# Query norm as the scale of the exponential, norm gains folded into k, one wide product for k's squares, in a two-layer trunk on one Trainium2 core

## The chip, the core and the metric

The kernel runs on one of the eight cores of a Trainium2 chip. A core has a matrix engine (TensorE, PE in the rows; its weight loads are the rows PEld), a vector engine (VectorE, DVE), a scalar engine (ScalarE, ACT), GpSimd (POOL) and SyncE (SP), which here only issues transfers. Each engine runs its own instructions in the order in which they were written, and they wait for each other at counting semaphores. Matrix products land in eight PSUM banks of 128 x 512 float32. The metric is the device time of one launch in microseconds (us), the median over runs.

## The reference, cut to what matters

Two residual layers over 512 tokens of width 1024. Layer 0 mixes tokens by a convolution module, layer 1 by differential attention; each is followed by a mixture of 32 gated-MLP experts (two experts for each token), whose weights, 6 MB for each expert and layer, are read from device memory. Everything is float32. The change is in the attention alone:

```
q = rms_norm(q.reshape(B, S, N_HEADS, 2, HEAD_DIM), q_g) * (HEAD_DIM ** -0.5)
k = rms_norm(k.reshape(B, S, N_HEADS, 2, HEAD_DIM), k_g)
s = einsum("bhcqd,bhckd->bhcqk", qb, kb)
p = softmax(where(mask, s, -inf), axis=-1)          # block-causal mask
a = p[:, :, 0] - lam * p[:, :, 1]
o = rms_norm(einsum("bhqk,bhkd->bhqd", a, vb), subln_g) * (1 - lambda_init)
```

There are 8 heads; each has two components (c = 0, 1) of 64 channels for q and k, and 128 channels of v. `rms_norm` divides each vector of 64 channels by the root of its mean square (plus 1e-6) and multiplies by a gain for each channel. For a fixed query the reciprocal root of q is one number for each row of scores.

## The kernel before

The span falls into these parts: layer 0's convolution (to about 300 us), its experts (to about 820), attention (840 to 1130), the output product with residual and routing (to 1210), layer 1's experts (to the end). In both expert parts the weights stream through a ring of six 2 MB units and four spare buffers. The stream is issued by SyncE: each unit's transfer waits for the semaphore of the work that last used its buffer. For layer 1's experts the first four units wait for `v_ready` and `qk_ready` of the attention (slots that held q, k, v weights); the next two and the first spare wait for the last `mix_ready`, the end of the output product; the rest follow the routing and the experts.

The attention is a software pipeline over 10 stages (`attention_steps()`): stage st projects q, k, v of head h = st, does scores, softmax and the weighted sum of head g = st - 1, and normalises the output of head e = st - 2. Stages 1 to 7 have both an h and a g; the scores of head 7 fall in stage 8, which has no projection and in its place runs part of the output product (`output_ahead`, L1474). The order on each engine is written out by hand; nothing is scheduled automatically.

On TensorE, a stage is: `scores(i)` for four query blocks i, i+1, i+2, i+3 of 128 rows (the widths are 128, 256, 384, 512 keys), with the four halves of the q and k projections (`qk_half`, L1380) between them; `transposed` (L1443) turns the combined probabilities `a`, which VectorE made, and `weighted` (L1454) multiplies them with v. `transposed(i + 3)` stands right behind `weighted(i + 2)`, then come `sum_squares` of k, half of v's projection (`v_half`, L1413), `spread_rs` (L1401), `weighted(i + 3)`, `output_T` (L1462), and the other half of v. Then the next stage begins with the scores of the head just projected, which wait for its normalised q and k (`qk_done`).

The norm of q and k goes like this. ScalarE squares the projected tile out of PSUM (channels are partitions, 512 tokens are columns) and copies it, times the gain, to SBUF (`qk_g_sb`, L734). TensorE sums the squares over channels with the squares as the stationary operand and two columns of `halves` as the moving one, four small products for each of q and k (L1391): the result has tokens as partitions, 128 x 16. ScalarE takes roots (L794), VectorE reciprocals (L1122). VectorE then widens the result to 128 x 512 (L1124), and TensorE turns it back to channels as partitions with eight products against the identity (`spread_rs`), so that VectorE can multiply (L1104).

The softmax of one query block goes: `maxima` (DVE, L1083: the negated row maximum of both components) gives `m_done`; ACT takes two exponentials with the maximum as bias and the row sum accumulated (L749); `combine` (DVE, L1089 to L1094) makes `a` from the two; PE transposes it.

Of the kernel before, what the change touches and what calls it, by code (L numbers as in the profile page):

```python
# [65 lines left out]
def trunk(nc, x, norm1_g, norm2_g, conv_w_in, conv_b_in, conv_dw, conv_dw_b, conv_ln_g, conv_ln_b,  # L66
# [11 lines left out]
    with ctx:  # L78
# [44 lines left out]
        def small_at(a, n=1):  # L123
# [26 lines left out]

        qk_ready, qk_sq, qk_ss, qk_root, qk_rec, qk_rs_ready, qk_scaled, qk_done = (
            sem("qk_ready"), sem("qk_sq"), sem("qk_ss"), sem("qk_root"), sem("qk_rec"), sem("qk_rs_ready"),
            sem("qk_scaled"), sem("qk_done"))
        v_ready, v_done = sem("v_ready"), sem("v_done")
# [111 lines left out]
        qk_sqb = [area1[:, c * T:(c + 1) * T] for c in range(2)]  # L266
        qk_rs_wide = [area1[:, (4 + c) * T:(5 + c) * T] for c in range(2)]
        qk_g_sb = [area1[:, (2 + c) * T:(3 + c) * T] for c in range(2)]
        p_sb = [scratch[:, b * 1024:(b + 1) * 1024].rearrange("p (c k) -> p c k", c=2) for b in range(3)]
# [5 lines left out]
        qk_bank = [bank[2], bank[3]]  # L275
        ss_bank = bank[4][:, 0:4 * NT]
        rs_bank = [bank[4], bank[1]]
        v_bank, aT_bank, o_bank = bank[5], bank[6], bank[7]
# [3 lines left out]
        o_ssq = scratch[:, 5280:5280 + 32]  # L282
        o_std = scratch[:, 5312:5312 + 32]
        o_r = scratch[:, 5344:5344 + 32]
        o_rn = scratch[:, 5376:5376 + 32]
        o_junk = scratch[:, 5408:5408 + P]
        qk_std = scratch[:, 5536:5536 + 4 * NT]
        qk_rs = scratch[:, 5552:5552 + 4 * NT]

# [311 lines left out]
        def _(act):  # L601
# [165 lines left out]
            for h, g, e in attention_steps():  # L767
                if g is not None:
                    i = NT * g
                    take_v(g)  # L770
                    probabilities(i)
                    take_aT(i)
                    probabilities(i + 1)
                if h is not None:
                    qk_square(h, 0)
                if g is not None:
                    take_aT(i + 1)
                    probabilities(i + 2)
                if e is not None:
                    o_squares(e)  # L780
                if g is not None:
                    take_aT(i + 2)
                    probabilities(i + 3)
                if h is not None:
                    qk_square(h, 1)
                if g is not None:
                    take_aT(i + 3)
                if e is not None:
                    act.wait_ge(o_sq, NT * (e + 1))
                    cols = slice(NT * e, NT * (e + 1))  # L790
                    a.activation(o_std[:, cols], o_ssq[:, cols], ACT.Sqrt, bias=eps[:], scale=1.0 / P).then_inc(on_std, 1)
                if h is not None:
                    act.wait_ge(qk_ss, 2 * (h + 1))
                    a.activation(qk_std, ss_bank, ACT.Sqrt, bias=eps[:], scale=1.0 / HEAD_DIM).then_inc(qk_root, 1)  # L794

# [6 lines left out]
        def _(dve):  # L802
# [263 lines left out]

            link(v.tensor_scalar(qk_g[:, 0:1], qk_g[:, 0:1], HEAD_DIM ** -0.5, None, ALU.mult))
            link(v.tensor_scalar(sub_g[:], sub_g[:], 1.0 - LAMBDA_INIT, None, ALU.mult))
# [11 lines left out]
            def maxima(i):  # L1080
                W = P * (pairs[i][1] + 1)
# [19 lines left out]

            def norm_qk(h, c):
                dve.wait_ge(qk_rs_ready, 2 * h + c + 1)
                v.tensor_tensor((qT, kT)[c][h % 2], qk_g_sb[c], rs_bank[c][:], ALU.mult).then_inc(qk_done, 1)  # L1104

            for h, g, e in attention_steps():
                if g is not None:
                    i = NT * g
                    maxima(i)
                    combine(i)  # L1110
                    maxima(i + 1)
                    combine(i + 1)
                    take_o(i)
                    maxima(i + 2)
                    combine(i + 2)
                    take_o(i + 1)
                    maxima(i + 3)
                    combine(i + 3)
                    take_o(i + 2)
                if h is not None:  # L1120
                    dve.wait_ge(qk_root, h + 1)
                    link(v.reciprocal(qk_rs, qk_std))  # L1122
                    for c in range(2):
                        v.tensor_copy(qk_rs_wide[c].rearrange("p (k f) -> p k f", f=HEAD_DIM),  # L1124
                                      qk_rs[:, 2 * NT * c:2 * NT * (c + 1)].unsqueeze(2).to_broadcast([P, 2 * NT, HEAD_DIM])
                                      ).then_inc(qk_rec, 1)
                if e is not None:
                    dve.wait_ge(on_std, e + 1)
                    cols = slice(NT * e, NT * (e + 1))
                    link(v.reciprocal(o_rn[:, cols], o_std[:, cols]))  # L1130
                    v.tensor_tensor(oh[e % 2], oh[e % 2], o_rn[:, cols].unsqueeze(2).to_broadcast([P, NT, P]),
                                    ALU.mult).then_inc(on_done, 1)
                if h is not None:
                    norm_qk(h, 0)
                if g is not None:
                    take_o(i + 3)
                if h is not None:
                    norm_qk(h, 1)
# [9 lines left out]
        def _(pe):  # L1148
# [223 lines left out]
            def qk_half(h, c, half):  # L1372

                u = n0 + 3 * (h // 4) + c
                if half == 0:
                    loaded(pe, u)
                    if h >= 1:
                        pe.wait_ge(qk_scaled, 2 * h - 1 + c)
                for k in range(4 * half, 4 * half + 4):
# [3 lines left out]

            def sum_squares(h, c):

                pe.wait_ge(qk_sq, 2 * h + c + 1)
                if c == 0 and h >= 1:
                    pe.wait_ge(qk_done, 2 * h - 1)
                for t in range(NT):
                    k = 2 * (NT * c + t)  # L1390
                    last = mm(ss_bank[:, k:k + 2], qk_sqb[c][:, t * P:(t + 1) * P], halves[:, 0:HEAD_DIM + 1:HEAD_DIM],  # L1391
                              start=True, stop=True)
                last.then_inc(qk_ss, 1)

            def spread_rs(h, c):

                pe.wait_ge(qk_rec, 2 * h + c + 1)
                if c == 1 and h >= 1:
                    pe.wait_ge(p_done, 2 * NT * h)
# [78 lines left out]
            for h, g, e in attention_steps():  # L1478
# [19 lines left out]
                if h is not None:  # L1498
                    qk_half(h, 1, 0)
                    sum_squares(h, 0)  # L1500
                if last_head:
# [15 lines left out]
                if h is not None:  # L1517
                    sum_squares(h, 1)
                    v_half(h, 0)
                if h is not None:  # L1520
                    spread_rs(h, 0)
                    spread_rs(h, 1)
                if last_head:
# [35 lines left out]
```

## Time and profile before

| | |
|---|---|
| median of 3 runs | 1717.74 us (1713.15 to 1719.24) |
| the profiled execution, device time | 1716.26 us |
| its span | 1714.5 us |
| mean granted TensorE clock | 0.919 of 2.4 GHz |
| PE matmul busy | 1420.8 us, 83% |
| DVE busy | 441.6 us, 26% |
| ACT busy | 328.2 us, 19% |
| the chain that ended last | PE 49%, DMA 33%, DVE 7%, POOL 4% |

The busy shares are averages over parts with different limits. The chain is read from the last instruction back to what released each step; its largest entries are the transfers of expert weights (31%) and the experts' first products (L1272, 19%), followed by the q and k projections of the attention (L1380, 7%). Ends of matmuls are modelled, so PE rows of a few hundredths of a microsecond are not exact.

### The profile page before, as it was taken

How to read it: one execution, taken by the hardware profiler on the slowest of the kernel's cores; microseconds unless marked ns; L12 is line 12 of the kernel's file. 1: busy time of each engine (PE TensorE's matmuls, PEld its weight loads, DVE VectorE, ACT ScalarE, POOL GpSimd, SP SyncE). 2: the span in 40 equal slices, each digit the busy share in tenths (PEclk: the TensorE clock that was granted, in tenths of full speed). 3: DMA queues.
4: the chain of work that ended last, by engine and by line, in shares of the span. 5: the costliest groups of instructions: out<-in, count | busy, mean ns of one | idle time of the engine just before them, and what ended most of it. 6: DMA issues, size and time to landing. Idle time of an engine off the chain costs nothing.

```text
span 1714.5 us, 17059 instructions
## 1 busy us (share of the span) xinstructions
PE 1420.8 (83%) x6028; PEld 645.3 (38%) x6028; DVE 441.6 (26%) x858; ACT 328.2 (19%) x629; POOL 278.0 (16%) x381
## 2 busy tenths in 40 slices
PE   4996696998888788887599999986997888888883
PEld 2442243332333233232376676644332322232331
DVE  1799614111110110110333333423211101101112
ACT  2555311010000000000334434421000000000000
POOL 0688100121111111110000000000121111111100
PEclk9998796999999899998799999987999999999997
DMA  9122005789999999998600400305799999999995
GB/s 337 21 98 98 1 37 239 294 363 418 421 420 420 420 420 419 418 416 335 247 1 1 148 1 2 147 25 230 309 365 420 420 419 421 419 418 416 414 414 205
DMA packets 91249, 473.13 MB, mean 276 GB/s; under 512 B 19675, under 2 KB 19675, under 8 KB 40260
## 3 DMA queue, kind: packets, MB, share of 16 engines
q1 hardware_dynamic: 78500, 443.12, 63.7%
q0 software_dynamic: 10400, 16.82, 2.6%
q10 hardware_dynamic: 2304, 12.58, 1.9%
q8 instruction: 29, 0.48, 0.1%
q14 instruction: 16, 0.13, 0.0%
HBM read 466.43 MB, written 23.33 MB: 286 GB/s over the span
## 4 chain that ended last, share of the span: by engine, by line
PE 49%; DMA 33%; DVE 7%; POOL 4%; issue 3%; SPq 3%; ACT 1%; ACTq 0%; POOLq 0%; DVEq 0%
DMA ring<-in_moe_w 31%; PE banks L1272 19%; PE banks L1380 7%; PE banks L1221 5%; POOL scratch L515 4%; PE banks L1289 3%; PE banks L1413 3%; SPq L315 2%; DVE banks L863 2%; PE banks L1170 2%; PE banks L1474 1%; PE banks L1427 1%; PE banks L1454 1%; DMA area<-y_dram 1%; PE banks L1239 1%
## 5 line engine op out<-in xcount | busy, mean ns | idle before, releaser
L1272 PE MATMUL banks<-ring,scratch 128*64 128x512 f32 x1984 | 503.6, 659 | 142.4 <-DMA ring<-in_moe_w 131.6
L1272 PEld LDWEIGHTS banks<-ring,scratch 128*64 128x64 f32 x1984 | 158.7, 150 | 483.5 <-issue 483.3
L1289 PE MATMUL banks<-ring,scratch 128*64 128x512 f32 x1008 | 231.7, 602 | 3.0 <-DVE scratch L1006 3.0
L1006 DVE COPY scratch<-banks 128x256 f32<-128x256 f32 x65 | 27.6, 425 | 799.7 <-PE banks L1280 799.7
L680 ACT ACTIVATE scratch<-banks 64x512 f32<-64x512 f32 x65 | 38.3, 589 | 597.6 <-PE banks L1272 597.6
L533 POOL COPY at_out<-rows_out 128x1 int32 (+1 forms) x64 | 11.7, 183 | 703.6 <-ACT scratch L684 703.6
L515 POOL TENSOR_TENSOR scratch<-scratch 128x512 f32<-128x512 f32 x88 | 112.0, 1273 | 62.0 <-ACT scratch L652 50.0
L1380 PE MATMUL banks<-hT,ring 128*128 128x512 f32 x256 | 117.9, 604 | 0.8 <-DVE hT L820 0.8
L1170 PE MATMUL banks<-hT,ring 128*128 128x512 f32 x256 | 112.5, 600 | 0.7 <-issue 0.7
L1289 PEld LDWEIGHTS banks<-ring,scratch 128*64 128x64 f32 x1008 | 68.4, 137 | 118.6 <-issue 111.6
L1221 PE MATMUL banks<-ring,area 128*128 128x512 f32 x200 | 99.0, 650 | 10.6 <-ACT area L662 9.6
L684 ACT ACTIVATE scratch<-banks 128x512 f32<-128x512 f32 x65 | 38.8, 597 | 285.8 <-PE banks L1289 285.8
L863 DVE SCALAR_TENSOR_TENSOR banks<-scratch,chan,banks 128x512 f32<-128x512 f32 x128 | 85.0, 750 | 0.0
L525 POOL DMA_INDIRECT scratch<-xn_dram,at_in x64 | 67.2, 1051 | 56.2 <-POOL at_in L522 53.9
L652 ACT ACTIVATE scratch<-scratch,chan 128x512 f32<-128x512 f32 x96 | 66.7, 718 | 49.1 <-POOL scratch L515 35.3
L543 POOL MEMSET scratch<- 128x512 f32 x4 | 2.1, 525 | 455.4 <-DVE x_res L892 455.3
L536 POOL DMA_INDIRECT y_dram<-scratch,at_out x64 | 65.8, 1028 | 56.5 <-POOL at_out L533 56.5
L1170 PEld LDWEIGHTS banks<-hT,ring 128*128 128x128 f32 x256 | 49.2, 193 | 62.7 <-issue 62.7
L1380 PEld LDWEIGHTS banks<-hT,ring 128*128 128x128 f32 x256 | 46.2, 189 | 49.5 <-issue 46.9
L1221 PEld LDWEIGHTS banks<-ring,area 128*128 128x128 f32 x200 | 40.1, 208 | 60.9 <-issue 56.0
L1413 PE MATMUL banks<-ring,hT 128*128 128x128 f32 x512 | 60.4, 276 | 0.0
L1158 PE MATMUL banks<-ident,area 128*128 128x128 f32 x128 | 26.1, 367 | 39.3 <-ACT area L624 34.3
(205 smaller groups left out, 1185.0 us busy)
## 6 DMA issues: line engine op xcount, KB each, us to landing
ring<-in_moe_w SPq DMA_DIRECT2D x374, 1024.0 KB, 17.1
area<-in_moe_w SPq DMA_DIRECT2D x12, 1024.0 KB, 14.7
ring<-in_attn_w_qkv SPq DMA_DIRECT2D x12, 1024.0 KB, 14.5
ring<-in_conv_w_in SPq DMA_DIRECT2D x8, 1024.0 KB, 14.6
area<-y_dram ACTq DMA_DIRECT2D x8, 1024.0 KB, 7.9
ring<-in_conv_w_out SPq DMA_DIRECT2D x4, 1024.0 KB, 12.4
xn_dram<-area ACTq DMA_DIRECT2D x8, 512.0 KB, 2.6
hT<-in_moe_w SPq DMA_DIRECT2D x4, 1024.0 KB, 12.4
```

The costliest lines, as they stand in the source:

```text
L515: g.tensor_tensor(pacc[ct % 2], pacc[ct % 2], tap[(k - 1) % TAP_BUFS], ALU.add).then_inc(tap_added, 1)
L525: g.indirect_dma_start(out=xe[s], out_offset=None, in_=xn_dram[l][:, :], in_offset=bass.IndirectOffsetOnAxis(ap=at_in[:, s:s + 1], axis=0) ...
L536: g.indirect_dma_start(out=y_dram[l][:, :], out_offset=bass.IndirectOffsetOnAxis(ap=at_out[:, s:s + 1], axis=0), in_=y_sb[s], in_offset=No ...
L652: a.activation(dst, u_buf[ct % 2][:, w:w + T], ACT.Copy, scale=chan[:, ct, w:w + 1]).then_inc(tap_made, 1)
L684: a.activation(y_sb[s], bank[6 + s][:], ACT.Copy).then_inc(sems["y_taken"], 1)
L863: ins = v.scalar_tensor_tensor(dst, ub[:, w:w + T], chan[:, ct, w:w + 1], acc, ALU.mult, ALU.add)
L1170: last = mm(dst, w[:, c, cols], src[:, c, :], start=start and c == 0, stop=stop and c == NC - 1)
L1221: last = mm(dst[:], src[:, c, t * P:(t + 1) * P], w_chunks(n0 + n)[:, c, :], start=c == 0, stop=c == NC - 1 and not bias)
L1272: last = mm(bank[2 + s][q * SLOTS:(q + 1) * SLOTS, :], xeT[s][:, j, h, :], w[:, c, :], start=c == 0, stop=c == NC - 1)
L1289: last = mm(bank[6 + s][q * SLOTS:(q + 1) * SLOTS, :], hidT[s][:, j, :], w2c[:, j, q * 512:(q + 1) * 512], start=j == 0, stop=j == 3)
L1380: last = mm(qk_bank[c][:], w_chunks(u)[:, k, (h % 4) * P:(h % 4 + 1) * P], hT[:, k, :], start=k == 0, stop=k == NC - 1)
L1413: last = mm(v_bank[:, t * P:(t + 1) * P], hT[:, k, t * P:(t + 1) * P], w_chunks(u)[:, k, (h % 4) * P:(h % 4 + 1) * P], start=k == 0, stop= ...
```

## The change

The two components of q are no longer normalised before the scores. Their reciprocal roots stay as a 128 x 8 tile with tokens as partitions (`q_rs`), where each column is the per-partition scale of one exponential; the negated maximum, which is the bias, has to be multiplied by the same number first. Both gains and the factor 1/8 go into one gain vector for k. The squares of k are summed by one product, with `halves` stationary and the 512 columns of squares moving, into the score bank 0; that result already stands in channels as partitions, spread over all 64 of each component, so nothing has to be widened or turned. ScalarE then takes 128 x 512 roots, VectorE 128 x 512 reciprocals, and one more VectorE instruction multiplies k out of PSUM by gain and reciprocal. `spread_rs` and `sum_squares` of k are gone.

```
 def qk_square(h, c):                                   # ACT
     act.wait_ge(qk_ready, 2 * h + c + 1)
     a.activation(qk_sqb[c], qk_bank[c][:], ACT.Square).then_inc(qk_sq, 1)
-    if h >= 1:
-        act.wait_ge(qk_done, 2 * h - 1 + c)
-    a.activation(qk_g_sb[c], qk_bank[c][:], ACT.Copy, scale=qk_g[:, c:c + 1]).then_inc(qk_scaled, 1)
+    if c == 0:
+        a.activation(qT[h % 2], qk_bank[0][:], ACT.Copy).then_inc(q_copied, 1)
...
 def probabilities(i):                                  # ACT
-        a.activation(p_sb[i % 3][:, c, 0:W], score[:, c, 0:W], ACT.Exp, bias=mx[:, i, c:c + 1],
+        a.activation(p_sb[i % 3][:, c, 0:W], score[:, c, 0:W], ACT.Exp, bias=mx_scaled[:, i % 4, c:c + 1],
+                     scale=q_rs[h % 2][:, 2 * b + c:2 * b + c + 1],
                      accum_out=ps[:, i, c:c + 1]).then_inc(p_done, 1)
...
-                    act.wait_ge(qk_ss, 2 * (h + 1))
-                    a.activation(qk_std, ss_bank, ACT.Sqrt, ...).then_inc(qk_root, 1)
+                    act.wait_ge(q_ss, h + 1)
+                    a.activation(q_std, q_ss_bank, ACT.Sqrt, ...).then_inc(q_root, 1)
+                    act.wait_ge(k_ss, h + 1)
+                    a.activation(k_std, k_ss_bank[:], ACT.Sqrt, ...).then_inc(k_root, 1)
...
 def maxima(i):                                         # DVE
-    v.tensor_reduce(mx[:, i, :], score[:, :, 0:W], AX.X, ALU.max, negate=True).then_inc(m_done, 1)
+    link(v.tensor_reduce(mx[:, i, :], score[:, :, 0:W], AX.X, ALU.max, negate=True))
+    v.tensor_tensor(mx_scaled[:, i % 4, :], mx[:, i, :], q_rs[h % 2][:, 2 * b:2 * b + 2], ALU.mult).then_inc(m_done, 1)
...
-def norm_qk(h, c):                                     # DVE
-    dve.wait_ge(qk_rs_ready, 2 * h + c + 1)
-    v.tensor_tensor((qT, kT)[c][h % 2], qk_g_sb[c], rs_bank[c][:], ALU.mult).then_inc(qk_done, 1)
+def scale_q(h):
+    dve.wait_ge(q_root, h + 1)
+    v.reciprocal(q_rs[h % 2], q_std).then_inc(q_rs_done, 1)
+
+def norm_k(h):
+    dve.wait_ge(k_root, h + 1)
+    link(v.reciprocal(k_rs, k_std))
+    v.scalar_tensor_tensor(kT[h % 2], qk_bank[1][:], qk_g[:, 1:2], k_rs, ALU.mult, ALU.mult).then_inc(k_done, 1)
...
-def spread_rs(h, c):                                   # PE
-    for t in range(NT):
-        last = mm(rs_bank[c][:, t * P:(t + 1) * P], qk_rs_wide[c][:, t * P:(t + 1) * P], ident[:], start=True, stop=True)
-    last.then_inc(qk_rs_ready, 1)
+def k_squares(h):
+    pe.wait_ge(qk_sq, 2 * h + 2)
+    pe.wait_ge(q_copied, h + 1)
+    mm(k_ss_bank[:], halves[:], qk_sqb[1], start=True, stop=True).then_inc(k_ss, 1)
...
 def scores(i):                                         # PE
     if b == 0:
-        pe.wait_ge(qk_done, 2 * (h + 1))
+        pe.wait_ge(q_copied, h + 1)
+        pe.wait_ge(k_done, h + 1)
...
                 if g is not None:
                     transposed(i + 3)
                 if h is not None:
-                    sum_squares(h, 1)
+                    k_squares(h)
                     v_half(h, 0)
-                if h is not None:
-                    spread_rs(h, 0)
-                    spread_rs(h, 1)
```

`link` makes VectorE wait for its own instruction. `q_squares(h)` is the old `sum_squares(h, 0)`.

The order on TensorE, in the second half of a stage. The kernel before (L1380 projections, L1454 weighted sums, L1443 transposes, L1391 sums of squares, L1413 v, L1401 `spread_rs`, L1462 output transposes, L1427 and L1431 the next stage's first scores with their mask):

```order
L1380 MATMUL banks_3<-hT,ring 128x512 x4
L1454 MATMUL banks_7<-area,scratch 128x128 x3
L1443 MATMUL banks_7<-ident,scratch 128x128 x4
L1391 MATMUL banks_5<-halves,area 128x2 x4
L1413 MATMUL banks_5<-ring,hT 128x128 x16
L1401 MATMUL banks_5<-ident,area 128x128 x4
L1401 MATMUL banks_1<-ident,area 128x128 x4
L1454 MATMUL banks_7<-area,scratch 128x128 x4
L1462 MATMUL banks_7<-ident,area 128x128 x4
L1413 MATMUL banks_5<-ring,hT 128x128 x16
L1427 MATMUL banks_1<-area 128x128 x2
L1431 MATMUL banks_1<-mask_col,mask_row 128x64 x2
```

And the same place in the changed kernel, whose line numbers have moved a little (L1383 projections, L1401 now the one wide product, L1412 v):

```order
L1383 MATMUL banks_3<-hT,ring 128x512 x4
L1454 MATMUL banks_7<-area,scratch 128x128 x3
L1443 MATMUL banks_7<-ident,scratch 128x128 x4
L1401 MATMUL banks_1<-area,halves 128x512
L1412 MATMUL banks_5<-ring,hT 128x128 x16
L1454 MATMUL banks_7<-area,scratch 128x128 x4
L1462 MATMUL banks_7<-ident,area 128x128 x4
L1412 MATMUL banks_5<-ring,hT 128x128 x16
L1427 MATMUL banks_1<-area 128x128 x2
L1431 MATMUL banks_1<-mask_col,mask_row 128x64 x2
```

Eight products against the identity and four small sums are gone, and one product of 128 x 512 stands in their place, ahead of v's first half.

The order on VectorE, from the last combination of a stage to the first combination of the next. Before (L1094 the combination, L1100 scaling of the output, L1122 and L1124 the reciprocals and their widening, L1130 and L1131 the output norm, L1104 the multiplication of q and of k, L1141 the output's gain, L1083 the row maximum):

```order
L1094 SCALAR_TENSOR_TENSOR scratch<-scratch 128x512
L1100 TENSOR_SCALAR area<-banks_7,scratch 128x128
L1122 RECIPROCAL scratch<-scratch 128x16
L1124 COPY area<-scratch 128x512 x2
L1130 RECIPROCAL scratch<-scratch 128x4
L1131 TENSOR_TENSOR area<-area,scratch 128x512
L1104 TENSOR_TENSOR area<-area,banks_5 128x512
L1100 TENSOR_SCALAR area<-banks_7,scratch 128x128
L1104 TENSOR_TENSOR area<-area,banks_1 128x512
L1141 TENSOR_SCALAR area<-banks_7,sub_g 128x512
L1083 TENSOR_REDUCE scratch<-banks_1 128x2
L1089 RECIPROCAL scratch<-scratch 128x1
```

The changed kernel at the same place (L1109 the reciprocal for q, L1113 and L1114 the norm of k, L1087 and L1088 the row maximum and its multiplication):

```order
L1099 SCALAR_TENSOR_TENSOR scratch<-scratch 128x512
L1105 TENSOR_SCALAR area<-banks_7,scratch 128x128
L1109 RECIPROCAL scratch<-scratch 128x8
L1135 RECIPROCAL scratch<-scratch 128x4
L1136 TENSOR_TENSOR area<-area,scratch 128x512
L1113 RECIPROCAL area<-area 128x512
L1114 SCALAR_TENSOR_TENSOR area<-banks_3,qk_g,area 128x512
L1105 TENSOR_SCALAR area<-banks_7,scratch 128x128
L1144 TENSOR_SCALAR area<-banks_7,sub_g 128x512
L1087 TENSOR_REDUCE scratch<-banks_1 128x2
L1088 TENSOR_TENSOR scratch<-scratch 128x2
L1094 RECIPROCAL scratch<-scratch 128x1
```

The widening copies and the two multiplications have given way to a reciprocal of the full 128 x 512 and one multiplication, both ahead of the last scaling of the output; and a small multiplication has come behind each row maximum.

## Rows read from the trace of the kernel before

**Rows 1.** Stretches: us; each engine's busy us (instructions); granted clock, DMA share, GB/s.
```profile
963.90:996.50 32.60, 32.60 (x188) 22.23 (x188) 12.64 (x32) 13.56 (x37) 0.00 (x0) 1.00 0.18 67
1094.50:1129.50 35.00, 32.91 (x119) 16.39 (x119) 12.10 (x30) 13.01 (x41) 0.00 (x0) 1.00 0.17 61
```

**Rows 2.** Waits of SyncE's queue: total us, times, longest us.
```profile
SPq L315 <- PE banks L1380: 232.3, 3, 115.6
```

**Rows 3.** The chain, whole span: start us, us, what.
```profile
1275.90 18.52 DMA ring<-in_moe_w
```

**Rows 4.** The chain inside stage 4, 963.9 to 996.5 us.
```profile
980.50 3.63 PE banks L1380 x8
984.80 0.51 PE banks L1443 x4
985.31 0.79 PE banks L1391 x8
...
989.78 1.79 PE banks L1401 x16
...
996.47 0.30 PE banks L1427
```

**Rows 5.** Timeline of ScalarE, stage 4: start us, us, what, [idle before, releaser].
```profile
964.45 1.28 ACT L749 ACT_TABLE_LOAD   x1
...
981.80 0.69 ACT L749 ACTIVATE scratch<-banks,scratch 128x512 f32<-128x512 f32 x1 [1.99 <-DVE scratch L1083]
...
985.35 0.60 ACT L765 ACTIVATE scratch<-banks 128x512 f32<-128x512 f32 x1
...
987.46 0.26 ACT L794 ACTIVATE scratch<-banks,eps 128x16 f32<-128x16 f32 x1
```

**Rows 6.** Timeline of ScalarE at the convolution's layer norm, 180 to 200 us.
```profile
186.90 0.72 ACT L659 ACTIVATE area<-area,eps 128x512 f32<-128x512 f32 x1 [3.42 <-DVE area L878]
...
192.49 0.81 ACT L662 ACTIVATE area<-area,chan 128x512 f32<-128x512 f32 x1 [3.57 <-DVE area L883]
```

**Rows 7.** Timeline of VectorE, stage 4.
```profile
964.42 0.42 DVE L1083 TENSOR_REDUCE scratch<-banks 128x2 f32<-128x256 f32 x1 [2.98 <-PE banks L1431]
...
966.85 0.27 DVE L1091 TENSOR_SCALAR scratch<-scratch,small 128x1 f32<-128x1 f32 x1
...
971.30 0.48 DVE L1094 SCALAR_TENSOR_TENSOR scratch<-scratch 128x256 f32<-128x256 f32 x1
...
980.54 1.22 DVE L1083 TENSOR_REDUCE scratch<-banks 128x2 f32<-128x1024 f32 x1 [1.19 <-PE banks L1431]
...
983.85 0.75 DVE L1094 SCALAR_TENSOR_TENSOR scratch<-scratch 128x512 f32<-128x512 f32 x1
...
988.92 0.69 DVE L1131 TENSOR_TENSOR area<-area,scratch 128x512 f32<-128x512 f32 x1
```

**Rows 8.** Timeline of VectorE just ahead of the attention.
```profile
841.89 0.16 DVE L1077 TENSOR_TENSOR small<-small 128x1 f32<-128x1 f32 x1 [0.27 <-ACT small L727]
```

**Rows 9.** Timeline of PE weight loads, stage 4.
```profile
967.56 0.14 PEld L1443 LDWEIGHTS banks<-ident,scratch 128*128 128x128 f32 x1 [0.38 <-DVE scratch L1094]
...
984.65 0.42 PEld L1443 LDWEIGHTS banks<-ident,scratch 128*128 128x128 f32 x4
```

**Rows 10.** Timeline of PE matmuls: stage 0, and the second transpose of stage 4.
```profile
855.98 1.05 PE L1391 MATMUL banks<-halves,area 128*128 128x2 f32 x8 [0.69 <-ACT area L731]
...
972.60 0.38 PE L1443 MATMUL banks<-ident,scratch 128*128 128x128 f32 x2
```

**Rows 11.** Timeline of VectorE at the convolution's layer norm, 187 to 192 us.
```profile
187.65 3.35 DVE L880 RECIPROCAL area<-area 128x512 f32<-128x512 f32 x1 [0.79 <-ACT area L659]
191.04 0.69 DVE L882 TENSOR_TENSOR area<-area 128x512 f32<-128x512 f32 x1
```

**Rows 12.** The page's costliest groups: count | busy us, mean ns | idle before.
```profile
L863 DVE SCALAR_TENSOR_TENSOR banks<-scratch,chan,banks 128x512 f32<-128x512 f32 x128 | 85.0, 750 | 0.0
```

**Rows 13.** ScalarE in stage 8: the wait ahead of the last probabilities' copy.
```profile
1118.84 0.60 ACT L765 ACTIVATE scratch<-banks 128x512 f32<-128x512 f32 x1 [5.46 <-PE banks L1443]
```

More of the change, by code:

```diff
@@ L149, in trunk @@
             sem("picks_done"), sem("ranks_ready"), sem("hot_done"), sem("lists_ready"), sem("lists_done"))
-        qk_ready, qk_sq, qk_ss, qk_root, qk_rec, qk_rs_ready, qk_scaled, qk_done = (
-            sem("qk_ready"), sem("qk_sq"), sem("qk_ss"), sem("qk_root"), sem("qk_rec"), sem("qk_rs_ready"),
-            sem("qk_scaled"), sem("qk_done"))
+        qk_ready, qk_sq, q_ss, k_ss, q_copied, q_root, k_root, q_rs_done, k_done = (
+            sem("qk_ready"), sem("qk_sq"), sem("q_ss"), sem("k_ss"), sem("q_copied"), sem("q_root"), sem("k_root"),
+            sem("q_rs_done"), sem("k_done"))
         v_ready, v_done = sem("v_ready"), sem("v_done")
@@ L266, in trunk @@
         qk_sqb = [area1[:, c * T:(c + 1) * T] for c in range(2)]
-        qk_rs_wide = [area1[:, (4 + c) * T:(5 + c) * T] for c in range(2)]
-        qk_g_sb = [area1[:, (2 + c) * T:(3 + c) * T] for c in range(2)]
+        k_rs = area1[:, 4 * T:5 * T]
+        k_std = area1[:, 2 * T:3 * T]
         p_sb = [scratch[:, b * 1024:(b + 1) * 1024].rearrange("p (c k) -> p c k", c=2) for b in range(3)]
@@ L275, in trunk @@
         qk_bank = [bank[2], bank[3]]
-        ss_bank = bank[4][:, 0:4 * NT]
-        rs_bank = [bank[4], bank[1]]
+        q_ss_bank = bank[4][:, 0:2 * NT]
+        k_ss_bank = bank[0]
         v_bank, aT_bank, o_bank = bank[5], bank[6], bank[7]
@@ L283, in trunk @@
         o_std = scratch[:, 5312:5312 + 32]
+        mx_scaled = scratch[:, 5560:5560 + 8].rearrange("p (i c) -> p i c", c=2)
+        q_std = scratch[:, 5552:5552 + 2 * NT]
         o_r = scratch[:, 5344:5344 + 32]
@@ L286, in trunk @@
         o_junk = scratch[:, 5408:5408 + P]
-        qk_std = scratch[:, 5536:5536 + 4 * NT]
-        qk_rs = scratch[:, 5552:5552 + 4 * NT]
+        q_rs = [scratch[:, 5536 + 2 * NT * b:5536 + 2 * NT * (b + 1)] for b in range(2)]
         ahead = (0, 4)
@@ L792, in _ @@
                 if h is not None:
-                    act.wait_ge(qk_ss, 2 * (h + 1))
-                    a.activation(qk_std, ss_bank, ACT.Sqrt, bias=eps[:], scale=1.0 / HEAD_DIM).then_inc(qk_root, 1)
+                    act.wait_ge(q_ss, h + 1)
+                    a.activation(q_std, q_ss_bank, ACT.Sqrt, bias=eps[:], scale=1.0 / HEAD_DIM).then_inc(q_root, 1)
+                    act.wait_ge(k_ss, h + 1)
+                    a.activation(k_std, k_ss_bank[:], ACT.Sqrt, bias=eps[:], scale=1.0 / HEAD_DIM).then_inc(k_root, 1)
             route(1)
@@ L1120, in _ @@
                 if h is not None:
[L1121 to L1126, printed above, removed]
+                    scale_q(h)
                 if e is not None:
@@ L1377, in qk_half @@
                     if h >= 1:
-                        pe.wait_ge(qk_scaled, 2 * h - 1 + c)
+                        pe.wait_ge((q_copied, k_done)[c], h)
                 for k in range(4 * half, 4 * half + 4):
@@ L1382, in qk_half, with q_squares @@
                     last.then_inc(qk_ready, 1)
[L1384 to L1388, printed above, removed]
+            def q_squares(h):
+                pe.wait_ge(qk_sq, 2 * h + 1)
+                if h >= 1:
+                    pe.wait_ge(q_root, h)
                 for t in range(NT):
-                    k = 2 * (NT * c + t)
-                    last = mm(ss_bank[:, k:k + 2], qk_sqb[c][:, t * P:(t + 1) * P], halves[:, 0:HEAD_DIM + 1:HEAD_DIM],
+                    last = mm(q_ss_bank[:, 2 * t:2 * t + 2], qk_sqb[0][:, t * P:(t + 1) * P], halves[:, 0:HEAD_DIM + 1:HEAD_DIM],
                               start=True, stop=True)
-                last.then_inc(qk_ss, 1)
-            def spread_rs(h, c):
-                pe.wait_ge(qk_rec, 2 * h + c + 1)
-                if c == 1 and h >= 1:
-                    pe.wait_ge(p_done, 2 * NT * h)
-                for t in range(NT):
-                    last = mm(rs_bank[c][:, t * P:(t + 1) * P], qk_rs_wide[c][:, t * P:(t + 1) * P], ident[:], start=True, stop=True)
-                last.then_inc(qk_rs_ready, 1)
+                last.then_inc(q_ss, 1)
+            def k_squares(h):
+                pe.wait_ge(qk_sq, 2 * h + 2)
+                pe.wait_ge(q_copied, h + 1)
+                mm(k_ss_bank[:], halves[:], qk_sqb[1], start=True, stop=True).then_inc(k_ss, 1)
             def v_half(h, half):
@@ L1499, in _ @@
                     qk_half(h, 1, 0)
-                    sum_squares(h, 0)
+                    q_squares(h)
                 if last_head:
```

9 lines of the change are left out of this document (4 added, 5 removed).

## The prediction, made before the changed kernel was run

> **What bounds the kernel now.** I read the whole span first: in the chain that ended last, transfers of expert weights hold the largest share and the matrix engine the next. So the first question is which of the two sets the time where the change is. The busy times by stretch answer it: stage 4 of the attention lasts 32.6 us and PE's matmuls are busy for 32.60 of them at clock 1.00, while DVE is busy for 12.64 and ACT for 13.56 [rows 1]. The attention's seven stages with both a projection and a softmax are a PE queue without gaps; an instruction taken out of it shortens the span by its own length, if nothing comes late instead.
>
> The second question is whether the time comes back further on. SyncE's queue waits 232.3 us in total, three times, for the q and k projections [rows 2]: the weight stream stands still in the attention, because its next buffers are held. All but four of layer 1's units start from the end of the output product or later, and the first wait of PE for a weight transfer in layer 1's experts is at 1275.90 [rows 3]. From there the stream sets the pace; it starts with the output product, so it moves with the attention's end. The four units that start inside the attention land before they are wanted, so they hide nothing.
>
> The third view is the chain inside a stage, for the price of each group as it stands on the path, and the fourth the timelines of ACT and DVE, to see what becomes late.
>
> **The change on PE.** `spread_rs` goes: 1.79 us a stage on the chain [rows 4]. `sum_squares` of k, 0.79 us [rows 4], goes too, but the wide product comes in its place. It has the shape of a projection product, 128 x 512 in float32, and four of these take 3.63 us [rows 4]: 0.91 us for one. So the wide product is no gain, it costs 0.12 us more than the four narrow ones. Bounds: 0.79 (no dearer than what it replaces), and 1.17 if its end isn't covered by the next product, as the group of L1391 shows 1.05 us as a duration beside 0.79 on the chain [rows 4, 10]. I take 0.91, the nearest shape. Net for each head: 1.79 - 0.12 = 1.67 us. Stage 0 has the same two edits, and its wait of 0.69 us for the squares [rows 10] stays. Eight heads: 13.4 us.
>
> **The change on the softmax chain.** Between row maximum and exponential stands a new multiplication of 128 x 2, linked to the one before. The nearest row, a small linked tensor-tensor, is 0.16 us [rows 8]; with the step of about 0.03 between linked instructions, 0.19 us. The dearest small one in the chain is 0.27 [rows 7], which gives the upper end 0.31; it can't be below 0.19 by much, since it is serial work.
>
> Each exponential gets a second per-partition operand, the scale beside the bias. The trace has no exponential with both. It has a 128 x 512 Sqrt with a bias operand in 0.72 us and a Silu with bias and scale operands in 0.81 [rows 6]: 0.09 more. The lower end is nothing, if the difference lies in the function. I take 0.09, twice per block, so 0.18. A block's combination is thus 0.37 us later (0.19 to 0.49).
>
> Who waits for it: the transposes. For the fourth block, the combination ends at 983.85 + 0.75 = 984.60 [rows 7] and the weight load of its transposes starts at 984.65 [rows 9]. There is 0.05 of slack, and everything on PE is queued behind it: the sum for k, v, the weighted sum, the next scores. So PE waits 0.32 us there, in stages 1 to 7: 2.2 us (1.0 to 3.1). For the second block the combination ends at 971.78 [rows 7] and its transposes start at 972.60 [rows 10]: 0.82 of slack covers 0.37, and the third has more. For the first block the loader waits for DVE already [rows 9]; but there the maximum is ready at 964.84 [rows 7] while ACT's table load runs until 965.73 [rows 5], so the multiplication is hidden, and only the 0.18 of the exponentials is left. The load, 0.14 long, then ends by 967.88, about when the products ahead of it end (the second block's scores follow without a gap), so I count nothing; exposed it would cost 7 x 0.18 = 1.3. In stage 8 ACT waits 5.46 us for the last block's transposes, which stand behind `output_ahead` [rows 13]: there the delay costs nothing.
>
> **The change on the k path.** In place of the small chain there is ACT root, DVE reciprocal, DVE multiplication, all 128 x 512, and the next scores wait for it. By stage 4, with PE 0.32 later from 984.65 on: the wide product starts at 985.63 and ends at 986.54. ACT copies the transposed block (0.60), loads the root's table (1.28), and reaches q's roots at 987.46 + 0.32 = 987.78 [rows 5]. That takes 0.26 [rows 5], then k's roots 0.60 to 0.72 [rows 5, 6], done by 988.7. DVE does the small reciprocals and the output norm, 0.69 [rows 7], until about 989.25. The reciprocal of 128 x 512 is the price to look up: 3.35 us [rows 11], until 992.6; the multiplication out of PSUM 0.75 [rows 12], until 993.4. PE reaches the next scores at 996.47 [rows 4] - 1.67 + 0.32 = 995.1. The margin is 1.7 us, so nothing is charged, and it holds in stage 0 too, where the squares are ready at 855.98 [rows 10] and v's two halves alone (3.6 us each) follow: k done at about 862.3, PE there at 864.1. DVE's last scaling of the output and the output's gain move behind the norm of k, to about 994.5; their readers on PE come after the next stage's first scores and projection quarter, at 999, and DVE's next maximum is wanted at 995.7. ACT loses one gain copy a stage. These I count at nothing, covered by the same 1.7 us.
>
> **Sum.** -13.4 + 2.2 = -11.2 us on the profiled execution's 1716.26: 1705.1. What lies outside its span, 1.8 us, stays. The median of the runs shown is 1.5 us above that execution, so a median should be between 1705.1 and 1706.6; I say 1706. With all ends: gain 8 x (1.79 + 0.79 - 1.17) - 3.1 = 8.2 at the least, 8 x 1.79 - 1.0 = 13.3 at the most, 1703 to 1708 from the profiled execution.
>
> **Rivals.** (A) The softmax chain becomes the bound in more places: the first block's 0.18 is exposed (1.3 us), the multiplication and the wide product are at their upper ends. Gain 8.2 - 1.3 = 6.9, time 1709 to 1711. For it: the loader already waits at the first block [rows 9] and the fourth has 0.05 us. Against: the values I took come from near shapes. (B) The gain at its upper end or past it: the exponential's second operand is free and the wide product is no dearer than the four: 1703. (C) The weight stream hides the gain: it would have to be running through the attention's end. Rows 2 and 3 speak against it; the time would be 1716 to 1718, and also if the change did not shorten PE's queue as its order shows.
>
> (D) Slower: a long Vector instruction holds its linked successor for about its own length again. The multiplication behind a 1.22 us maximum [rows 7] would start 1.22 later, which is 7 x 1.22 = 8.5 us on PE, and k's multiplication 3.35 later, which passes the margin of 1.7 by 1.65 in 8 stages, 13.2 us. Sum -11.2 + 8.5 + 13.2 = +10.5: 1727. It decides as soon as the gap behind the reciprocal passes 1.7 us; with both it is slower than before when they add over 11.2 us. Against it: the reciprocal that starts at 187.65 and lasts 3.35 ends at 191.00, and its linked successor starts at 191.04 [rows 11]. The Trainium skill, page "VectorE: DVE Perf Modes", section "The DRAIN you can't avoid", speaks for this rival, if its drain is taken to lie behind the duration in the rows: it says that each Vector instruction is followed by a drain of about its duration less 266 ns, and that the next can't start until the pipe is empty. By its figure the gaps would be 0.96 and 3.09 us, and the sum, as an estimate from that page, 1723. The rows just named disagree with that reading, 0.04 us against 3.09, so the chance is small.
>
> **How the numbers follow.** Forecast 0.60, A 0.21, B 0.10, C 0.05, D 0.04. About 0.5%, 8.6 us, is what a measurement can tell from no change; that bound lies at 1709.1. The forecast and B lie beyond it but for the spread of the runs, which is 3 us either way; A lies on it. Faster by over 0.5%: 0.72; within: 0.23; slower: 0.05. The likeliest case alone is 1702 to 1710. The range adds A and the spread: 1700 to 1713.
>
> **What would show it.** Right: stages 1 to 7 of 31.3 us, L1401 as one product with two records of 0.45 on the chain, the reciprocal L1113 at 3.35, the next scores without a wait for L1114, PE's loader waiting for L1099 at the fourth block by about 0.3. Exponentials of 512 in 0.77. Wrong: PE idle ahead of the scores with releaser L1114 (k's path), a stage of 31.8 or more with waits for L1099 (rival A), or the attention 11 us shorter while the end of the span does not move (C).

## The result and the profile after

The changed kernel takes 1708.41 us (median of 9 runs, 1704.09 to 1711.11), the kernel before 1717.74 (9 runs, 1712.93 to 1721.85). The ratio is 0.9939, 95% interval 0.9925 to 0.9954: 10.5 us less (7.9 to 12.9); the two medians by themselves lie 9.3 us apart. Two more measurements of the same pair gave 0.9934 (0.9918 to 0.9949) and 0.9934 (0.9916 to 0.9951). The profiled execution took 1709.75 us with a span of 1708.0. Of the runs further down, one of the twelve executions of `q_only` took 3935 us and is left out of its ratio.

The stretches of the changed kernel, in the columns of [rows 1]: stage 4 of the attention, then the beginning of its stage 0.

```profile
961.30:992.60 31.30, 31.07 (x167) 20.08 (x168) 14.96 (x34) 14.27 (x38) 0.00 (x0) 1.00 0.23 89
...
842.00:855.00 13.00, 12.83 (x29) 5.82 (x29) 1.59 (x9) 1.29 (x3) 0.00 (x0) 0.83 0.53 196
```

Stage 4 is 31.2 us from scores to scores and was 32.7; PE is no longer busy for all of it, 0.23 us are missing (ends of matmuls are modelled; by the starts of the products, below, the wait is 0.38). The second row is explained further down: the granted clock is 0.83 there.

The chain inside stage 4 of the changed kernel (start us, us, what) answers to [rows 4]:

```profile
977.87 0.17 PE banks L1431 x2
978.04 0.02 issue
978.06 1.24 DVE scratch L1087
979.30 0.02 issue
979.32 0.17 DVE scratch L1088
979.50 0.03 issue
979.52 1.64 ACT scratch L749 x4
...
981.75 0.76 DVE scratch L1099
982.51 0.04 issue
982.56 0.66 PE banks L1443 x4
983.21 0.86 PE banks L1401 x2
984.07 3.57 PE banks L1412 x32
987.65 0.89 PE banks L1454 x8
```

Before, this chain held PE's instructions alone. Now it leaves PE behind the fourth block's scores, runs through row maximum, multiplication, exponentials and combination, and comes back at the transposes (L1443): the softmax of the fourth block has become the limit for 4.5 us of the stage, most of which PE spends on products that end 0.38 us too early. The 0.38 is read from starts (PE's timelines, before and then after, with the weight load of the transposes in the changed kernel):

```profile
983.97 0.83 PE L1454 MATMUL banks<-area,scratch 128*128 128x128 f32 x6
984.66 0.66 PE L1443 MATMUL banks<-ident,scratch 128*128 128x128 f32 x4
```
```profile
981.49 0.83 PE L1454 MATMUL banks<-area,scratch 128*128 128x128 f32 x6
982.56 0.66 PE L1443 MATMUL banks<-ident,scratch 128*128 128x128 f32 x4 [0.23 <-DVE scratch L1099]
```
```profile
982.55 0.42 PEld L1443 LDWEIGHTS banks<-ident,scratch 128*128 128x128 f32 x4 [0.42 <-DVE scratch L1099]
```

The transposes started 0.69 us behind the start of the weighted sum ahead of them, and now start 1.07 behind it. Their weight load, which now waits, starts 0.05 us behind the combination's end (981.75 + 0.75 = 982.50). Behind the transposes stands the wide product with 0.86 us in place of 0.79, and nothing between v's first half and the weighted sum. `spread_rs` and its 1.79 us are gone.

ScalarE in the same stage (timeline), against [rows 5]:

```profile
979.52 0.78 ACT L749 ACTIVATE scratch<-banks,scratch 128x512 f32<-128x512 f32 x1 [2.19 <-DVE scratch L1088]
...
983.25 0.60 ACT L766 ACTIVATE scratch<-banks 128x512 f32<-128x512 f32 x1 [0.96 <-PE banks L1443]
983.87 1.28 ACT L792 ACT_TABLE_LOAD   x1
...
985.37 0.25 ACT L795 ACTIVATE scratch<-banks,eps 128x8 f32<-128x8 f32 x1
985.52 0.68 ACT L797 ACTIVATE area<-banks,eps 128x512 f32<-128x512 f32 x1
```

VectorE (timeline), against [rows 7] and [rows 11]:

```profile
979.32 0.16 DVE L1088 TENSOR_TENSOR scratch<-scratch 128x2 f32<-128x2 f32 x1
...
981.75 0.75 DVE L1099 SCALAR_TENSOR_TENSOR scratch<-scratch 128x512 f32<-128x512 f32 x1
...
986.53 3.35 DVE L1113 RECIPROCAL area<-area 128x512 f32<-128x512 f32 x1
989.92 0.75 DVE L1114 SCALAR_TENSOR_TENSOR area<-banks,qk_g,area 128x512 f32<-128x512 f32 x1
```

And PE at the next stage's first scores, the other place where it could wait.

```profile
992.48 0.49 PE L1427 MATMUL banks<-area 64*128 64x128 f32 x4
```

The exponential takes 0.78 us and took 0.69. The Trainium skill, page "ScalarE: Activation LUTs", section "What ACT_TABLE_LOAD costs", has about 93 ns for each operand of this kind; this trace agrees, with 0.09. The norm of k ends at 989.92 + 0.75 = 990.67, and PE comes to the scores at 992.48 without a wait: a margin of 1.8 us.

**Where the time went**, from the traces of the kernel before and of the changed one in us: the attention's start is 1.8 later (842.17 against 840.40, nothing of the change is ahead of it); stage 0 lasts 25.84 against 25.60; stages 1 to 7 last 218.14 against 228.41, so 10.3 less; from there to the first wait for a weight transfer it is 182.7 against 181.5; from that wait to the end 439.2 against 438.6. The sum is the 6.5 us between the spans. Only the attention's stages are of the change; the rest is what executions of one kernel differ in. In three executions of the changed kernel stages 1 to 7 lasted 218.13, 218.14 and 218.14 us, while the start lay between 841.01 and 842.88 and the stretch to the first weight wait between 179.3 and 182.8. Most of that spread has a cause in the traces: PE's clock. Here are 12 us of the output product, 42 us behind the end of stage 7, in the first profile of the changed kernel and in `after_again`, in the columns of [rows 1]:

```profile
1128.15:1140.15 12.00, 12.00 (x31) 7.53 (x30) 2.23 (x4) 2.59 (x4) 0.00 (x0) 0.51 0.19 75
```
```profile
1126.80:1138.80 12.00, 12.00 (x48) 7.24 (x47) 2.89 (x5) 2.59 (x4) 0.00 (x0) 0.93 0.19 75
```

In the one the granted clock stays at 0.51, in the other it is back at 0.93. The first weight wait then comes 182.7 us behind stage 7, or 179.3. The one profile of the kernel before is of the slower kind (0.57 at this place, 181.5 us).

The first weight wait moved with the attention's end, from 1275.90 [rows 3] to:

```profile
1268.83 17.88 DMA ring<-in_moe_w
```

### The profile page after: what moved, and what is told of

It is laid out like the page before. It is cut to its first block, busy times and chain, and to the rows that moved or that the text cites. A ratio compares the mean times of both kernels' runs of the same rounds, so it can differ in the third digit from the quotient of the medians.

```text
span 1708.0 us, 16725 instructions
## 1 busy us (share of the span) xinstructions
PE 1409.3 (83%) x5852; PEld 628.0 (37%) x5852; DVE 460.6 (27%) x874; ACT 333.2 (20%) x629; POOL 277.5 (16%) x381
## 4 chain that ended last, share of the span: by engine, by line
PE 47%; DMA 33%; DVE 8%; POOL 4%; issue 3%; SPq 3%; ACT 2%; ACTq 0%; POOLq 0%; DVEq 0%
DMA ring<-in_moe_w 31%; PE banks L1275 19%; PE banks L1383 5%; PE banks L1224 5%; POOL scratch L516 4%; PE banks L1292 3%; PE banks L1412 3%; SPq L316 2%; DVE banks L866 2%; PE banks L1173 2%; PE banks L1474 1%; PE banks L1427 1%; DMA area<-y_dram 1%; PE banks L1242 1%; DMA area<-in_conv_b_out 1%
## 5 line engine op out<-in xcount | busy, mean ns | idle before, releaser
L1383 PE MATMUL banks<-hT,ring 128*128 128x512 f32 x256 | 119.9, 613 | 0.8 <-DVE hT L823 0.8
L1383 PEld LDWEIGHTS banks<-hT,ring 128*128 128x128 f32 x256 | 47.0, 193 | 50.8 <-issue 48.1
L1412 PEld LDWEIGHTS banks<-ring,hT 128*128 128x128 f32 x512 | 59.0, 192 | 3.8 <-issue 3.8
```

Source lines behind the costliest of these rows:

```text
L1383: last = mm(qk_bank[c][:], w_chunks(u)[:, k, (h % 4) * P:(h % 4 + 1) * P], hT[:, k, :], start=k == 0, stop=k == NC - 1)
L1412: last = mm(v_bank[:, t * P:(t + 1) * P], hT[:, k, t * P:(t + 1) * P], w_chunks(u)[:, k, (h % 4) * P:(h % 4 + 1) * P], start=k == 0, stop= ...
```

## The experiments

**The changed kernel again**, unedited, beside the two runs after it.

> The changed kernel once more, beside the next two. Ratio to the kernel before 0.993 to 0.995; stages 1 to 7 of 31.2 us. If its first attention stage runs at full clock in this execution, stage 0 (first projection to first scores) lasts 23.8 us and not 25.9.

Measured: 1706.71 us, ratio 0.9934. Stages 31.22 to 31.23, stage 0 23.78 us. PE in stage 0 of this execution and of the first one (timelines):

```profile
842.88 10.57 PE L1383 MATMUL banks<-hT,ring 128*128 128x512 f32 x24 [0.78 <-DVE hT L823]
```
```profile
842.17 12.63 PE L1383 MATMUL banks<-hT,ring 128*128 128x512 f32 x24 [0.78 <-DVE hT L823]
```

The same twelve products take 10.57 us in one execution and 12.63 in another. In the first profile the granted clock was 0.83 over 842 to 855 us; in this one 1.00. Just before the attention, over 839 to 842 us, PE was busy for 2.1 to 2.8 of 3 us at a granted clock of 0.50 to 0.53. Over the next 3 us the clock was 1.00 in the one and still 0.50 in the other, which came to 1.00 behind 848. The kernel before has 10.57 us for these products too. So stage 0's edits are read at like clock: 23.78 against 25.60, 1.82 us less (the other stages give the same number, 32.67 against the 30.85 of `no_scale` below), and the attention as a whole is 12.1 us shorter.

**The extra work on the softmax chain, taken out.** `no_scale` leaves out the query norm, both the operand and the multiplication; `scale_only` has the operand (ones) and no multiplication.

```
-    link(v.tensor_reduce(mx[:, i, :], score[:, :, 0:W], AX.X, ALU.max, negate=True))
-    v.tensor_tensor(mx_scaled[:, i % 4, :], mx[:, i, :], q_rs[...], ALU.mult).then_inc(m_done, 1)
+    v.tensor_reduce(mx_scaled[:, i % 4, :], score[:, :, 0:W], AX.X, ALU.max, negate=True).then_inc(m_done, 1)
...
-                                 scale=q_rs[h % 2][:, 2 * b + c:2 * b + c + 1],
+                                 scale=ones[:, 0:1],      # scale_only; no_scale has no such line
```

> The changed kernel with the query norm left out: the exponential has no scale operand and the maximum is not multiplied. Theory (both additions together delay the fourth block's combination by 0.37 us): exponentials of 512 at 0.69 us, stages of 30.85 us, no wait of PE for the combination beyond 0.05.

> As the one before, the query norm left out, but the exponential has a scale operand that holds ones; the maximum is not multiplied. Theory (the second operand costs 0.09 us in each exponential): exponentials of 512 at 0.78, combination 0.18 later, slack 0.05, so stages of 31.0 us, between 30.85 and 31.23. Rival (the multiplication alone makes the wait, since exponentials overlap): 30.85. Rival (the operand makes it all): 31.2.

Measured, one stage of each in the columns of [rows 1], `no_scale` first:

```profile
954.28:985.13 30.85, 30.85 (x165) 20.01 (x165) 14.42 (x30) 13.53 (x37) 0.00 (x0) 1.00 0.24 96
```
```profile
960.07:991.10 31.03, 31.00 (x166) 20.02 (x166) 14.41 (x30) 14.24 (x37) 0.00 (x0) 1.00 0.23 93
```

And an exponential of 512 in each (ScalarE's timelines):

```profile
972.36 0.69 ACT L749 ACTIVATE scratch<-banks,scratch 128x512 f32<-128x512 f32 x1 [1.99 <-DVE scratch L1086]
```
```profile
978.14 0.78 ACT L749 ACTIVATE scratch<-banks,scratch,ones 128x512 f32<-128x512 f32 x1 [1.99 <-DVE scratch L1087]
```

30.85, 31.03 and 31.23 us: the second operand costs 0.18 us a stage, the multiplication 0.20, together 0.38, or 2.7 us in seven stages. Both rivals, that one of the two makes all of it, fall. Without the two PE is busy for all of the stage again. The single times, 1696.07 and 1704.83 us, carry the variation outside the attention and are not used.

**The two parts of the change, each alone.** `q_only` has the scale in the exponential and k's old path; `k_only` the reverse. Core of the edits against the changed kernel:

```
 # q_only: k's squares by four narrow products, then
+    def widen_k(h):                                        # DVE
+        link(v.reciprocal(k_r8, k_std))
+        v.tensor_copy(k_rs as 128 x 8 x 64, k_r8 spread over 64).then_inc(k_rec, 1)
+    def spread_k(h):                                       # PE, behind v_half(h, 0)
+        last = mm(k_rs_bank[:, t * P:(t + 1) * P], k_rs[:, t * P:(t + 1) * P], ident[:], start=True, stop=True)
+    v.tensor_tensor(kT[h % 2], k_g_sb, k_rs_bank[:], ALU.mult)
...
 # k_only: no scale and no multiplication in the softmax, and for q
+    v.tensor_copy(q_wide as 128 x 8 x 64, q_rs spread over 64).then_inc(q_rec, 1)
+    last = mm(bank[4][:, t * P:(t + 1) * P], q_wide[:, t * P:(t + 1) * P], ident[:], start=True, stop=True)
+    v.tensor_tensor(qT[h % 2], q_sb, bank[4][:], ALU.mult).then_inc(q_done, 1)
```

> Only the query part of the change: q's reciprocal roots are the scale of the exponential; k is normalised as before, by narrow sums, a widened tile and four products against the identity. Theory: PE loses half of the identity products, 0.89 us a head, and pays the wait of 0.38 us for the longer softmax tail in stages 1 to 7: stages of 32.2 us, 4.5 us less than the kernel before (ratio 0.9974). Rival (the longer softmax tail costs nothing by itself): 7.1 us less, stages of 31.8.

> Only the key part of the change: wide product, roots and reciprocals of 128 x 512; q is normalised as before by a widened tile and four identity products, and the exponential has no scale. Theory: 0.89 us of identity products go, the wide product costs about what the narrow ones did, no wait at the fourth block: stages of 31.8 us, 7.3 us less than the kernel before (ratio 0.9957). Rival (the k path is late, since a widening copy and q's multiplication share VectorE with the reciprocal): a wait of PE for the norms ahead of the scores, stages over 32.

Measured: `q_only` 1710.73 us, ratio 0.996 (0.9945 to 0.9975); `k_only` 1706.90 us, ratio 0.9935 (0.9917 to 0.9953). One stage of each:

```profile
959.40:991.55 32.15, 31.92 (x179) 21.42 (x178) 12.28 (x35) 14.40 (x38) 0.00 (x0) 1.00 0.20 77
```
```profile
963.80:995.54 31.74, 31.74 (x174) 20.90 (x173) 15.48 (x32) 13.53 (x37) 0.00 (x0) 1.00 0.22 82
```

Stages 1 to 7 are 3.77 us shorter in `q_only` (224.64 against 228.41) and 6.50 in `k_only` (221.91). Their sum is 10.27, which is what the whole change gives: the two parts act on PE's queue independently. The combination's wait, 0.23 us in PE's row, is in `q_only` and not in `k_only`. Neither rival holds. By its time `k_only` is 11.2 us faster (8.1 to 14.3), as much as the whole change, by its trace 7.4 in the attention; `q_only` 6.9 (4.3 to 9.5) and 4.7. The times don't tell the parts from the whole, since they carry the stretch behind the attention as well (178.8 us in the trace of `k_only`, 181.5 in that of the kernel before). The traces are the finer measure here.

**The margin of k's path.** One line more:

```
     link(v.reciprocal(k_rs, k_std))
+    link(v.reciprocal(k_rs, k_std))
```

> The 128 x 512 reciprocal of k's roots is done twice, 3.39 us more on the path of k. Theory (margin of 1.8 us ahead of the next scores): a wait of 1.6 us in each of 8 stages for the norm of k, stages of 32.8 us, 12.7 us more than the changed kernel, so about 2 us over the kernel before. Rival (the k path already limits the stage in part, margin near zero): 3.4 us in each stage, 27 us more. Rival (the path is far from deciding): no more than 2 us more in all.

Measured: 1725.99 us, ratio 1.0049 (1.0031 to 1.0067), slower than the kernel before by 8.4 us, where 2 were expected. The wait is as expected, 1.60 us in each stage, and stages without anything else last 32.90. But stages 4, 5 and 7 last 34.60, and stage 8 loses as much at its start. PE at the start of stages 3, 4 and 8 (timeline), and the granted clock (seventh value) in five stretches; the last but one follows the wait of stage 5, the last that of stage 6:

```profile
929.94 0.49 PE L1428 MATMUL banks<-area 64*128 64x128 f32 x4 [1.60 <-issue]
...
930.52 3.70 PE L1384 MATMUL banks<-hT,ring 128*128 128x512 f32 x8
...
962.84 0.49 PE L1428 MATMUL banks<-area 64*128 64x128 f32 x4 [1.60 <-issue]
...
963.42 5.40 PE L1384 MATMUL banks<-hT,ring 128*128 128x512 f32 x8
...
1100.11 5.40 PE L1475 MATMUL banks<-ring,area 128*128 128x512 f32 x8
```
```profile
962.90:965.60 2.70, 2.70 (x10) 1.35 (x11) 1.57 (x7) 1.26 (x5) 0.00 (x0) 0.74 0.98 401
965.60:968.30 2.70, 2.70 (x6) 1.10 (x5) 0.52 (x2) 0.00 (x0) 0.00 (x0) 0.63 0.87 364
968.30:971.00 2.70, 2.70 (x12) 1.16 (x11) 0.85 (x2) 0.60 (x2) 0.00 (x0) 1.00 0.03 12
...
998.10:1000.80 2.70, 2.70 (x4) 1.20 (x5) 1.49 (x7) 0.99 (x4) 0.00 (x0) 0.54 0.00 0
...
1032.10:1034.80 2.70, 2.70 (x11) 1.40 (x12) 1.57 (x7) 1.25 (x5) 0.00 (x0) 1.00 0.02 6
```

Eight times PE waits 1.5 to 1.6 us, ahead of stages 1 to 8. Behind four of these waits the granted clock falls towards 1.2 GHz, behind the other four it stays at 2.4. Where it falls, the next four products take 1.70 us longer than their 3.70. A transfer beside them is not the cause: at stage 4 one runs (DMA share 0.98), at stage 5 none does (0.00). What decides it, no run here shows. Waits of 12.7 us and falls of 6.8 make 19.5; the medians are 19.3 apart. So the margin is what was read (3.39 added, 1.6 of it seen as a wait, 1.8 covered), both rivals fall, and a gap of that size costs PE up to twice its length. The expected 12.7 us were short by the falls of the clock.

**Work for the wait.** The seven waits at the fourth block can be filled: four of v's products are put ahead of the transposes.

```
+                if h is not None:
+                    v_part(h, 0, range(0, 4))
                 if g is not None:
                     transposed(i + 3)
                 if h is not None:
                     k_squares(h)
-                    v_half(h, 0)
+                    v_part(h, 0, range(4, NC))
+                    v_part(h, 1, range(0, NC))
```

> Four of the sixteen products of v's first half stand ahead of the fourth block's transposes, so that PE has 0.9 us of work while the combination ends. Theory (the softmax tail costs 0.38 us a stage as a wait of PE): no wait for L1099 at the fourth block, stages 1 to 7 of 30.85 us, 2.7 us less than the changed kernel (ratio to the kernel before 0.9925). k is ready 0.5 us later and the margin ahead of the next scores falls from 1.8 to 1.3 us without a wait. Rival (the wait is not what the stage pays for, it is covered in the PE queue): stages stay at 31.2 us.

Measured: 1699.81 us, ratio 0.9889 (0.9871 to 0.9906), against 0.9934 of the changed kernel beside it. PE in stage 4, and VectorE's combination and norm of k there (timelines):

```profile
979.61 0.83 PE L1465 MATMUL banks<-area,scratch 128*128 128x128 f32 x6
980.28 1.06 PE L1411 MATMUL banks<-ring,hT 128*128 128x128 f32 x8
981.17 0.60 PE L1454 MATMUL banks<-ident,scratch 128*128 128x128 f32 x4
981.61 1.02 PE L1401 MATMUL banks<-area,halves 128*128 128x512 f32 x2
...
990.15 0.49 PE L1438 MATMUL banks<-area 64*128 64x128 f32 x4
```
```profile
979.87 0.75 DVE L1099 SCALAR_TENSOR_TENSOR scratch<-scratch 128x512 f32<-128x512 f32 x1
...
988.48 0.75 DVE L1114 SCALAR_TENSOR_TENSOR area<-banks,qk_g,area 128x512 f32<-128x512 f32 x1
```

The wait is gone, and stages last 30.77 us. That is 0.45 less and not 0.38: the first half of v takes 3.57 us in both, but the transposes take 0.44 from start to next start in place of 0.49, and the weighted sum ahead of them 0.67 in place of 0.69. Stages 1 to 7 last 214.97 us, 3.2 less than 218.14. k is ready at 989.23 for scores at 990.15, a margin of 0.9 where 1.3 was expected: the expectation had moved k's path and forgotten that the stage ends earlier as well. The gain in time was over twice that of the trace; the pair measured again:

> The changed kernel beside the next one on the same chip. Ratio to the kernel before 0.9935 (the attention is 12.1 us shorter when its first stage has the same clock, less what the executions vary).

> The early first quarter of v's products again, since the first measurement lay 6.9 us under the changed kernel, while the stages of its trace account for 3.2 us. Theory (only the seven waits are gone): 3.2 us less than the changed kernel run beside it, ratio to the kernel before 0.9915, stages of 30.77 us. Rival (the shorter attention is worth more further on, in the weight stream): 6 us or more again.

Measured: 1706.77 us, ratio 0.9934 (0.9916 to 0.9951); and 1700.95 us, ratio 0.9898 (0.9880 to 0.9916). The early products beat both kernels in both measurements. Of the 5.8 to 6.9 us by which its medians lie under the changed kernel's, 3.2 are accounted for by the stages. Neither of the two traces of this version shows a shorter stretch behind the attention than the shortest of the changed kernel: 179.5 and 179.2 us to the first weight wait against 182.7, 179.3 and 182.8, and 439.5 and 439.4 from there to the end against 439.2, 439.6 and 438.5. Both traces of this version are of the kind in which the clock comes back early behind stage 7 (0.92 and 0.93 at the place shown above), and so is one of three of the changed kernel. A difference in that is worth up to 3.4 us, where 2.6 to 3.7 are not accounted for. Whether the early return comes more often in this version stays open, and so neither the 3.2 us of the theory nor the 6 or more of its rival is settled by the times.

## Why the prediction was right, point by point

- **The bound.** PE's queue sets the attention's time, and the weight stream moves with its end. Shown: what an edit of PE's queue was expected to do to a stage is measured there to 0.1 us in every kernel run, but for the three stages of the doubled reciprocal in which the clock fell. And while stages 1 to 7 range from 215.0 to 234.9 us over the kernels, the stretch from the first weight wait to the end stays at 437.9 to 439.6.
- **`spread_rs` and the wide product.** Foretold 1.67 us a head net. The wide product took 0.86 and not 0.91, v's first half came out 0.09 shorter (3.57 against 3.66 from its start to the next group), and net it is 1.82, read in stage 0, where no other edit acts. This term was 0.15 a head too small, 1.2 us in all. That the wide product gains nothing over four narrow ones was right: 0.86 against 0.79.
- **The softmax tail.** Foretold: multiplication 0.19, operands 0.18, slack 0.05, wait 0.32. Measured 0.20 and 0.18, and a wait of 0.38; the slack was not there. The 0.05 that was read as slack, from the combination's end (984.60) to the weight load (984.65), is the same 0.05 that the changed kernel shows where the load does wait (982.50 to 982.55): it is the step from one to the other. 2.7 us in place of 2.2. The first block's 0.18 was not exposed, as said: `no_scale` and `scale_only` differ by 0.18 a stage, once and not twice. Stage 8 took 35.14 us from its first scores to the first product behind it, and 35.08 before, so it paid 0.06.
- **The k path.** Foretold ready at 993.4 with PE at 995.1, a margin of 1.7; measured 1.8, and the doubled reciprocal confirmed it with waits of 1.6. The 989.25 from which the forecast counts the reciprocal is in no row (the row that it names ends at 989.61, before the widening is taken out); measured, moved to the same start of the stage, it was 989.0.
- **The sum.** Foretold stages of 31.3 us, measured 31.23. Foretold a median of 1706 us, measured 1708.4, inside the 1700 to 1713. Foretold 11.2 us in all; the traces show 12.1 in the attention, the times 10.5 (7.9 to 12.9) and twice 11.3. The first execution's slow clock in stage 0, 2.1 us, is of the size of that difference, but how often it comes in the kernel before was not counted. Two of the terms were off in opposite directions, by 1.2 us and 0.5; that the stage came out within 0.1 us is in part luck.
- **The rivals.** (A) needed the first block exposed: it was not. (B) went too far, since the second operand costs what the Silu row showed and the wide product is 0.07 dearer than the four. (C) is refuted by the first weight wait, which moved from 1275.9 to 1268.8. (D): the linked multiplication starts 0.04 us behind the reciprocal's end (986.53 + 3.35, then 989.92), now in the attention itself, and the multiplication behind the 1.24 us maximum likewise, 0.02 us; so that reading of the drain in the Trainium skill, page "VectorE: DVE Perf Modes", section "The DRAIN you can't avoid", does not hold here.

## What to carry to other kernels

Where one engine's queue has no gaps, the worth of an edit is the length that leaves that queue, less what the edit adds to the shortest slack of any chain that comes back to it. That slack is found at the instruction whose operand is ready when its turn comes: here it was nothing at the fourth block's transposes, where 0.38 us of work on two lightly loaded engines cost 0.38 on the busy one. A step of 0.05 us between the releaser's end and the waiting load is not slack. Such a wait is cheap to fill with independent work from behind it, and a path with a margin (1.8 us for the reciprocal of 3.35) should be read to its end before anything is added to it.

## What the runs showed of the hardware that was not expected

An idle time of 1.60 us on TensorE, every 33 us or so, was followed by a lower granted clock in four cases of eight (0.54 to 0.74 in the stretches shown) and by none in the other four; each fall cost 1.7 us more. The eight waits thus cost 13 us as waits and 7 as clock. And the return to full clock came at different times in executions of one kernel: behind the stretch at 0.50 ahead of the attention, worth 2.1 us (10.57 against 12.63 us for the same products), and behind stage 7, worth 3.4 us (179.3 against 182.7 us to the first weight wait).
